# A fused two-block kernel: one weight load moved ahead of the small loads, a norm's weights loaded in place, and three reorderings around the second block's norms

## The reference, cut to what matters

```python
# first block
h = x
xn = rms_norm(h, norm1_g);  proj = xn @ w_in          # q k v qi ki wi su sv ga gb
... # rope, indexed sparse attention, spatial gating, gates, merged @ w_out
h = h + hier_moe(rms_norm(h, norm2_g), ...)            # 32 experts
x = rms_norm(h, norm_f_g)
# second block
z = rmsnorm(x, ln1_2) @ w_in_2
... # three kinds of attention, three gates
x = x + merged @ w_o_2
h2 = rmsnorm(x, ln2_2)
x = x + (silu(a) * b) @ w_down_2                       # a, b = conv(h2 @ w_up_2)
out = rmsnorm(x, ln_f_2)
```

## Time and profile before

| | us |
|---|---|
| median of 3 runs | 936.77 (935.92 to 937.26) |
| the profiled execution's own time | 937.57 |
| its span in the profile | 935.8 |

### The profile page before, as it was taken

The page is one execution under the profiler, slowest core; times in us unless marked ns, Lnnn a source line. Parts: engine busy times, 40 slices in busy tenths (PEclk is TensorE's granted clock), DMA queues, the critical chain, the costliest instruction groups (busy, mean ns, idle before and its releaser), DMA issues.

```text
span 935.8 us, 14702 instructions
## 1 busy us (share of the span) xinstructions
PE 838.4 (90%) x5971; PEld 696.9 (74%) x5971; DVE 494.3 (53%) x771; ACT 387.1 (41%) x526; POOL 92.3 (10%) x111
## 2 busy tenths in 40 slices
PE   3899999799999986866678899999999899999996
PEld 3889789799998632312332599898898799999995
DVE  5799577654464411100110475555657657676584
ACT  5333453364333321011111554455553466556462
POOL 1032000111000000000000501212151000000000
PEclk9899999899999999988898999999999999999998
DMA  7756555225489999999999985525444735646611
GB/s 221 258 159 224 183 180 181 91 91 180 165 338 393 381 423 423 421 422 422 421 422 410 261 174 180 179 93 180 94 177 144 239 126 180 232 137 205 199 46 46
DMA packets 94392, 217.55 MB, mean 232 GB/s; under 512 B 14664, under 2 KB 45510, under 8 KB 82050
## 3 DMA queue, kind: packets, MB, share of 16 engines
q1 hardware_dynamic: 93649, 215.32, 63.9%
q10 hardware_dynamic: 576, 1.18, 0.4%
q0 software_dynamic: 112, 0.30, 0.3%
HBM read 215.44 MB, written 1.34 MB: 232 GB/s over the span
## 4 chain that ended last, share of the span: by engine, by line
PE 58%; DMA 16%; DVE 13%; ACT 5%; issue 3%; SPq 3%; DVEq 0%; POOL 0%; ACTq 0%
DMA moe_ring<-in_w_expert_in 14%; PE ps L831 14%; PE ps L833 13%; PE ps L832 13%; PE ps L1253 6%; PE ps L1169 5%; DVE w_lo L1631 3%; DMA stage<-in_w_in 1%; DVE w_odd L1631 1%; DMA stage_b<-in_w_up 1%; SPq L699 1%; ACT w_hi L1334 1%; ACT w_odd L1334 1%; PE ps L1201 1%; PE ps L1191 1%
## 5 line engine op out<-in xcount | busy, mean ns | idle before, releaser
L833 PE MATMUL ps<-x_hi,w_lo 128*128 128x256 f32 x664 | 189.0, 285 | 0.0
L833 PEld LDWEIGHTS ps<-x_hi,w_lo 128*128 128x128 f32 x664 | 128.6, 194 | 0.0
L1631 DVE TENSOR_TENSOR w_lo<-stage,w_hi 128x2048 fp32r<-128x2048 f32 (+1 forms) x44 | 101.8, 2355 | 31.1 <-ACT w_hi L1334 29.8
L831 PE MATMUL ps<-x_hi,w_hi 128*128 128x256 f32 x360 | 104.8, 291 | 8.0 <-DVE w_lo L1631 7.4
L1334 ACT ACTIVATE w_hi<-stage 128x2048 fp32r<-128x2048 f32 (+1 forms) x44 | 79.1, 1849 | 58.6 <-PE ps L833 50.4
L832 PE MATMUL ps<-x_lo,w_hi 128*128 128x256 f32 x360 | 103.1, 286 | 0.0
L831 PE MATMUL ps<-x_hi,w_odd 128*128 128x256 f32 x312 | 89.6, 287 | 1.3 <-DVE x_lo L1622 1.3
L832 PE MATMUL ps<-x_lo,w_odd 128*128 128x256 f32 x312 | 89.0, 285 | 0.0
L833 PE MATMUL ps<-x_hi,w_odd 128*128 128x256 f32 x312 | 88.9, 285 | 0.0
L831 PE MATMUL ps<-x_hi,w_lo 128*128 128x256 f32 x304 | 86.3, 284 | 0.0
L832 PE MATMUL ps<-x_lo,w_lo 128*128 128x256 f32 x304 | 86.0, 283 | 0.0
(11 more groups left out here) (387 smaller groups left out, 1916.5 us busy)
## 6 DMA issues: line engine op xcount, KB each, us to landing
stage<-in_w_in SPq DMA_DIRECT2D x23, 2048.0 KB, 7.9
moe_ring<-in_w_expert_in SPq DMA_DIRECT2D x44, 1024.0 KB, 18.5
moe_ring<-in_w_expert_out SPq DMA_DIRECT2D x20, 1024.0 KB, 16.8
stage_b<-in_w_up SPq DMA_DIRECT2D x12, 1024.0 KB, 7.8
stage<-in_w_down SPq DMA_DIRECT2D x11, 1024.0 KB, 5.1
stage<-in_w_up SPq DMA_DIRECT2D x10, 1024.0 KB, 9.5
up_odd<-in_w_expert_in SPq DMA_DIRECT2D x8, 1024.0 KB, 21.0
down_odd_a<-in_w_expert_out SPq DMA_DIRECT2D x6, 1024.0 KB, 21.8
```

The lines of the kernel that those rows point to most:

```text
L831: mm(out, still[0], moving[0], start=first, stop=False)
L833: return mm(out, still[1], moving[0], start=False, stop=last)
L1631: tt(lo[:, cols], staged(n)[:, cols], hi[:, cols].bitcast(fp32), ALU.subtract).then_inc(lo_ready, 1)
```

## The change

1. SyncE loads the vector rows, then issues the load of unit 2 (its wait for unit 0's split in front), and only then the other small loads.
2. `norm2_g` is loaded straight into 128 partitions (`gain2`, runs of 4 elements) instead of into rows to be transposed; the router's weights and the gathered expert inputs read it there. `vec` 1 and 2 come after `relbias`.
3. The turns of the angles are computed on GpSimd, after its powers of the first norm.
4. At the seam, the second token tile is scaled in two halves, and ScalarE does `between(0)` after `raw_hi`, not ahead of it.
5. At `norm` 3 the residual of tile 0 goes ahead of tile 0's transposes, that of tile 1 between the two tiles' transposes. VectorE does the second half of the feed-forward unit's split after the last fill's result.

```diff
@@ schedule()
     steps.extend(unit("kiwi", 0, [0]))
-    at("vec", 1)
-    at("vec", 2)
     steps.extend(unit("qi", 0, [0, 1]))
     at("wit")
     at("relbias")
+    at("vec", 1)
+    at("vec", 2)
...
-    steps += [{"op": "ffsplit"}, fills[0], {"op": "normtile", "i": 3}, fills[1], {"op": "norm", "i": 3}]
+    steps += [{"op": "ffsplit", "half": 0}, fills[0], {"op": "normtile", "i": 3}, fills[1], {"op": "ffsplit", "half": 1},
+              {"op": "norm", "i": 3}]
@@ SyncE
-                for s in range(2):
-                    eng.dma_start(rows_a[16 + 4 * s:20 + 4 * s], a["norm2_g"][0, s * BANK:(s + 1) * BANK].rearrange("(p k) -> k p", k=4),
-                                  allow_slow_non_contiguous=True).then_inc(vec_in, 16)
-                eng.dma_start(rows_b, a["conv_w_2"][0, 1:3].rearrange("w (f p) -> (w f) p", p=P)).then_inc(vec_in, 16)
+                eng.dma_start(rows_b, a["conv_w_2"][0, 1:3].rearrange("w (f p) -> (w f) p", p=P)).then_inc(vec_in, 16)
+
+            def small_loads():
+                for s in range(2):
+                    eng.dma_start(gain2[:, 4 * s:4 * s + 4], a["norm2_g"][0, s * BANK:(s + 1) * BANK].rearrange("(p k) -> p k", k=4)).then_inc(gain2_in, 16)
...
                 if n == STAGES:
-                    small_loads()
+                    row_loads()
                 if n >= STAGES:
                     wait_split(eng, n - STAGES)
                 load(n)
+                if n == STAGES:
+                    small_loads()
@@ TensorE
             def norm(i):
                 for t in range(NT):
                     if i == 2:
                         eng.wait_ge(scaled, t + 1)
+                    elif i == 3:
+                        residual_into_psum(t)
+                        eng.wait_ge(xs_ready, 3 + t)
...
+                        if i == 2 and (t, k) == (1, KT // 2):
+                            eng.wait_ge(scaled, 3)
...
-                    if t == 0 and i == 3:
-                        residual_into_psum()
@@ ScalarE
                         if s["half"] == 0:
                             split(s["unit"], 0)
-                            between(0)
...
                     norm(s["i"])
                     if s["i"] == 2:
+                        between(0)
                         split(units_one + 1, 1)
@@ VectorE
-                if i == 0:
-                    turns_of_angles()
...
-                gain = vec[:, C_G2:C_G2 + KT].unsqueeze(2)
+                eng.wait_ge(gain2_in, 32)
+                gain = gain2.unsqueeze(2)
...
-                tt(h_tok[:, 1, :], ps[:, 6:8, :].rearrange("p b n -> p (b n)"), wide_g[:, :], ALU.mult).then_inc(scaled, 1)
+                eng.wait_ge(scaled, 1)
+                for hf in range(2):
+                    half = slice(hf * BANK, (hf + 1) * BANK)
+                    tt(h_tok[:, 1, half], ps[:, 6 + hf, :], wide_g[:, half], ALU.mult).then_inc(scaled, 1)
@@ GpSimd
+            def turns_of_angles():
+                eng.wait_ge(pos_in, 32)
+                pos_f = k_feat[:, 5, :]
+                step(eng.tensor_copy(pos_f, pos_i))
+                for k in range(2):
+                    step(eng.tensor_scalar(ang[:, k, :], pos_f, freq[:, k:k + 1], None, ALU.mult))
+                magic = 12582912.0
+                step(eng.tensor_scalar(turns, ang, float(1 / (2 * np.pi)), magic, ALU.mult, ALU.add))
+                step(eng.tensor_scalar(turns, turns, magic, None, ALU.subtract))
+                eng.sem_inc(turns_ready, 1)
```

More of the change, by code:

```diff
@@ L923, in fill_at @@
                 if kind == "vec":
-                    eng.wait_ge(*((gain_in, 16) if i == 0 else (vec_in, 16 * 8)))
-                    src, r = ((rows_a[0:8, :], 8), (rows_a, P), (rows_b, 88))[i]
+                    eng.wait_ge(*((gain_in, 16) if i == 0 else (vec_in, 16 * 6)))
+                    src, r = ((rows_a[0:8, :], 8), (rows_a[0:120, :], 120), (rows_b, 88))[i]
                     last = eng.transpose(ps[:, bank, 0:r], src, ident[0:r, 0:r])
@@ L1096, in route, with residual_into_psum @@
                 residual(1, 1)
-            def residual_into_psum():
-                for b in range(4):
+            def residual_into_psum(t):
+                for b in (2 * t, 2 * t + 1):
                     fills = sum(1 for s in steps[:steps.index(cur)] if s["op"] == "at" and s["n"] % 4 == b)
                     eng.wait_ge(at_free[b], fills)
[L1103 to L1108, removed]
+                eng.wait_ge(h_ready, 7 + t)
+                for hf in range(2):
+                    mm(ps[:, 4 + 2 * t + hf, :], ident[:, :], h_tok[:, t, hf * BANK:(hf + 1) * BANK],
+                       start=True, stop=False, skip_group_check=True)
             def norm(i):
@@ L1303, in between @@
             def between(t):
-                eng.wait_ge(scaled, t + 1)
+                eng.wait_ge(scaled, (1, 3)[t])
                 act(junk[:, t, :], ps[:, 4 + 2 * t:6 + 2 * t, :].rearrange("p b n -> p (b n)"), ACT.Square,
@@ L1313, in norm @@
                         squares_of(i, t)
-                g0 = (C_G1, C_G2, C_LN1, C_LN2)[i]
+                g0 = (C_G1, None, C_LN1, C_LN2)[i]
                 if i == 0:
@@ L1556, in _ @@
                 elif s["op"] == "ffsplit":
-                    ff_split_up(0, 0)
+                    if s["half"] == 0:
+                        ff_split_up(0, 0)
                 elif s["op"] == "norm":
@@ L1581, in _ @@
                     eng.wait_ge(rstd_ready, 2)
-                    eng.wait_ge(scaled, 4)
+                    eng.wait_ge(scaled, 5)
                     act(y_tok[:, 1, BANK:D], h_tok[:, 1, BANK:D], ACT.Copy, scale=rstd[:, 1:2]).then_inc(y_ready[1], 1)
@@ L1638, in split_tiles, with ff_split_up @@
                 tt(lo[:, f:f + 2, :], src[:, f:f + 2, :], hi[:, f:f + 2, :].bitcast(fp32), ALU.subtract).then_inc(dve_split, 1)
-            def ff_split_up(u, p):
-                for half in range(2):
+            def ff_split_up(u, p, halves=range(2)):
+                for half in halves:
                     eng.wait_ge(ff_hi, u * 2 + half + 1)
@@ L1645, in ff_split_up @@
                     tt(lo[:, cols], ff_stage(p)[:, cols], hi[:, cols].bitcast(fp32), ALU.subtract).then_inc(ff_lo, 1)
-            def turns_of_angles():
-                eng.wait_ge(pos_in, 32)
-                pos_f = k_feat[:, 5, :]
-                step(eng.tensor_copy(pos_f, pos_i))
-                for k in range(2):
-                    last = ts(ang[:, k, :], pos_f, freq[:, k:k + 1], None, ALU.mult)
-                step(last)
-                magic = 12582912.0
-                step(ts(turns, ang, float(1 / (2 * np.pi)), magic, ALU.mult, ALU.add))
-                step(ts(turns, turns, magic, None, ALU.subtract))
             def angles():
+                eng.wait_ge(turns_ready, 1)
                 two_pi = 2 * np.pi
@@ L1674, in vectors @@
             def vectors(i):
-                c, f0, f1 = ((0, 0, 8), (0, 8, P), (P, 0, 88))[i]
+                c, f0, f1 = ((0, 0, 8), (0, 8, 120), (120, 0, 88))[i]
                 n = where["vec", i]
@@ L1838, in copy_gathered @@
                     eng.wait_ge((gather_a, gather_b)[half], it + 1)
-                    g2 = vec[:, C_G2 + 4 * half:C_G2 + 4 * half + 4].unsqueeze(2).broadcast_to([P, 4, P])
+                    g2 = gain2[:, 4 * half:4 * half + 4].unsqueeze(2).broadcast_to([P, 4, P])
                     tt(xg[p][:, 4 * half:4 * half + 4, :], ps[:, half, :].rearrange("p (k c) -> p k c", k=4), g2,
@@ L2142, in last_norm @@
                 eng.wait_ge(pow_ready, 7 + t)
-                eng.wait_ge(scaled, 3 + t)
+                eng.wait_ge(scaled, 4 + t)
                 one = slice(t, t + 1)
@@ L2158, in _ @@
                 elif s["op"] == "ffsplit":
-                    ff_split_up(0, 0)
+                    ff_split_up(0, 0, (s["half"],))
                 elif s["op"] == "norm":
@@ L2230, in _ @@
                         power(before + t + 1, slice(t, t + 1))
+                    if i == 0:
+                        turns_of_angles()
                 elif s["op"] == "between":
```

13 lines of the change are left out of this document (7 added, 6 removed).

## The result

| | median us | runs | ratio to before, 95% interval |
|---|---|---|---|
| changed kernel | 928.92 (927.97 to 930.05) | 4 | 0.9913, 0.9895 to 0.9932 |
| before, beside it | 937.01 (935.92 to 938.36) | 4 | |
| changed kernel again, in a later job | 929.57 (929.46 to 929.89) | 5 | 0.9923, 0.9909 to 0.9936 |

The change makes the kernel 8 us faster by the first ratio (6.4 to 9.8) and 7 by the second. The forecast was 927.5 with a range of 924.8 to 931.5. The profiled execution of the changed kernel has an own time of 929.64 and a span of 927.9, so that the two spans differ by 7.9.

The account below looks back on a forecast made before the run. The prediction took TensorE, busy nine tenths of the span, as the bound, its idle time being what can be won. 5.8 (start) + 3.5 (seam) + 0 (`norm` 3) = 9.3 us off gave 928.3, 927.5 as a median; range 924.8 to 931.5.

Parts of the forecast that it names:

- Part A: Start: earlier unit 2 load, moved copies and angles let unit 3 end near 60.3, saving 5.8 us (4.4 to 7.6).
- s: Start: shift of everything behind the first norm from moving angle work to GpSimd, taken as 1.0 us (0 to 1.5).
- rival 2: Start: GpSimd holds VectorE up, so the angles' shift is 0; time 928.5 to 928.9, chance 0.10.
- Part B: Seam: `raw_hi` earlier saves 1.85 us, and no slow clock spell behind the shorter gap 1.65: 3.5 (1.5 to 3.6).
- rival 1: Seam: the slow clock spell stays, so the seam gains only 1.85 us; time 929.1, chance 0.18.
- Part C: `norm` 3: residual order's 0.65 us gain is lost as VectorE's split delays GpSimd's power; 0 (-0.5 to +0.65).
- Rivals 3, 4 and 5: Expert part takes start's gain back, 933.3 (0.08); unit 2's load not sooner, 930 to 932 (0.05); relative-bias tables late, slower (0.03).

Follow-up runs that it names:

- start-only kernel: Kernel before with only the start's edits (loads, `gain2`, place of `vec` 1 and 2, angles on GpSimd): 931.78 us, ratio 0.9958.
- the angles' run: Changed kernel with the turns of the angles back on VectorE ahead of the first Newton step: 930.07 us, ratio 0.9925.
- The parts alone: Kernel before with one part each: start edits 0.9958; seam edits 0.9967; `norm` 3 edits 1.0016 (931.78, 932.68, 937.05 us).
- the copies on ScalarE: Changed kernel, unit 3's split earlier, indexer-weight and `vec` 1 and 2 copies on ScalarE, both first feed-forward split halves ahead of `norm` 3: 925.93 us, ratio 0.9885.
- the split ahead alone: Changed kernel with unit 3's split put ahead of the indexer-weight, relative-bias, router-weight and `vec` copies: 927.96 us, ratio 0.9908.
- residual-only kernel: Changed kernel with both halves of the first feed-forward split back ahead of `norm` 3: 928.04 us, ratio 0.9918; again 928.72, 0.9914.
- load-behind run: Changed kernel with unit 2's load issued behind all small loads again, `norm2_g` staying in place: 929.43 us, ratio 0.9922.

## Why the prediction was right, and where it was not

- **Part A, 5.8: the size was off, 4.12.** VectorE decides, as said, and its chain ended 5.17 earlier, at 50.41 and not 49.8: 0.86 from s (1.0 forecast), 5.25 from the load and the copies (5.4), less 0.39 for the copies' return (0.6), and less 0.55 for the split of unit 2, stretched to 5.04 beside GpSimd's sum; that term was missing. The other 1.05 is the lag behind VectorE: 10.48 before and in the start-only kernel, 11.53 here, because of the slow stretch from 49 to 53. I had forecast a gap of 1 to 2 us there and no slow stretch; the gap was 2.67. Unit 3 ended at 61.94, just inside the 62 past which the prediction called itself wrong.
- **The cause in part A was half named.** "It may be issued when unit 0 is split" is true and worth nothing beside the other edit: with `norm2_g` in place the load behind everything is in time. The step that failed is "`norm2_g` in place saves descriptors on a queue that then has slack, and reading the gain from another buffer costs nothing: both 0": its first half is enough for all that the prediction gave to the load's place. That the load's place alone would not have been enough isn't shown.
- **s** was 0.64 at TensorE's first product of unit 0 (15.12 against 15.76 before) and 0.86 on VectorE's rotation of `kiwi`; by the angles' run 0.5 of it reaches the end of unit 3. The prediction took s as 0 at the Trainium skill's full lock (SBUF — State Buffer, SBUF: two separate sides). Here VectorE's first two splits were stretched (1.71 against 1.29) by less than the GpSimd work beside them, and on GpSimd the last of two instructions of one size took 1.81 against 0.62, but the gain did not go to 0, and the measurement decides; rival 2 falls. At `norm` 3, where GpSimd's instruction ended with the split (727.24 and 727.18), the trace agrees with the lock.
- **Part B, 3.5: right,** 1.90 and 1.55. The slow stretch at the seam was there in all 3 profiles of the old seam and in none of the 11 of the new one; rival 1 falls for this gap.
- **Part C, 0: the mechanism was right and the price wrong.** The power took 1.16 (0.9 forecast), held up until VectorE's split ended, and the way was 0.16 longer. What the step left out is the clock: two gaps of 1.27 and 1.28 with the eight transposes between them had a slow stretch that cost 1.46 us behind them in all 7 profiles, and none of the 7 kernels without the moved split had one there. Without the moved split the residual products keep most of the 0.65 that was forecast for them: the way takes 26.44 to 26.68 in the four profiles with them and 26.99 to 27.22 in the three with the old order.
- **Rivals 3, 4 and 5.** The expert part kept the 4.12; the load and the tables were early enough. The stretch from 60 us to the seam, here counted from the end of unit 4, was as long as before within 1 us: 439.01 against 439.40.
- **The sum was near partly by luck.** From 9.3, part A took 1.7 and part C 1.6 in the profiled execution, while the slow stretch near 600 that was absent and the expert part gave 1.95 back: 7.9. The parts alone make 3.9+3.1-1.5=5.5 by their ratios and 4.6+3.7-0.6=7.7 by their medians; with intervals of 1 to 1.3 us on each side of each, that does not show whether they simply add.

## What to carry to other kernels

A transfer that is late may be late because of the issues ahead of it on its queue, not of its own place: price those first. When a wait is removed, add up the next engine's work to the end of the stage and use the measured lag behind it; moving one item in that engine's order gives little, and giving it to an idle engine gives nearly all of it (unit 4 ended 1.31 earlier with the copies on ScalarE than with the split ahead alone). Two profiles can differ by slow stretches of the clock that belong to no edit, so cut both spans at common events and look for steps of one size before explaining a difference.

## What was not expected of the hardware

- The same kernel has a slow stretch behind the same gap in one execution and not in another: the residual-only kernel had none behind its gap of 2.71 at 48.41, and one behind its gap of 2.66 at 48.45. TensorE by stretch in the two executions:

```profile
49.00:51.00 2.00, 1.56 (x14) 1.00 0.06 9
```
```profile
49.00:51.00 2.00, 2.00 (x11) 0.50 0.06 9
...
595.00:597.00 2.00, 2.00 (x11) 0.50 0.98 371
```

  In the eight profiles with a gap of 2.44 to 2.72 there, four had it. The Trainium skill (TensorE: Matmul & The Clock Gate, What's actually happening) says that the hardware's looks are not tied to the kernel's start; that the same gap is caught once and not the other time agrees with it. A slow stretch costs 1.4 to 1.6 us where TensorE bounds, and 0.8 to 1.05 in unit 3, where some of it falls on a wait.
- Two transfers of 512 single four-byte elements together held SyncE's queue for 5.87 us, and the 2 MB load of unit 2, issued later on that queue, took 12.5 us to land; in the load-behind run it took 10 at most. In runs of 16 bytes the two took 0.85 to 1.05.
- A GpSimd instruction on one column took 0.19 us, and 1.16 beside a VectorE subtraction of two SBUF tiles that had begun before it. It ended 0.06 behind the subtraction, which was not longer for it (2.29, as before). At the old seam the 2.63 of the earlier trace rows ended at 536.97, and two such subtractions that VectorE had begun at 532.44 ended at 536.92.
